# Four edits of order in a one-core decoder layer: first norm, last attention pair, loads of x, start of the down product

## The reference, cut to what matters

```python
q, k, v, hc, bc, cc = split(rms_norm(x, g_mix) @ w_in)      # 1024 columns each
q, k = rms_norm(q, q_norm), rms_norm(k, k_norm)             # per head of 64
attn = merged dilated attention of 16 heads, with a bias by distance
y = bc * short_conv(cc * hc)                                # three taps
h = x + concat(rms_norm(attn), rms_norm(y)) @ w_out
h = h + (silu(n @ w_gate) * (n @ w_up)) @ w_down            # n = rms_norm(h), width 5632
h = h + sigmoid(rms_norm(h) @ w_ple_gate) * (p @ w_ple_proj)
```

## Time and profile before

| what | value |
|---|---|
| median of 3 runs | 2536.05 us (2533.64 to 2537.11) |
| profiled execution | 2535.68 us, span 2534.1 us |
| TensorE busy | 2481.5 us, 98% of the span |
| DVE / ACT / POOL busy | 69% / 37% / 10% |
| mean granted TensorE clock | 0.992 of full speed |
| chain that ended last | PE 93%, DVE 3%, DMA 2%, issue 1%, ACT 1% |
| DMA | 324 MB, mean 128 GB/s |

### The profile page before, as it was taken

The page is one execution under the profiler, slowest core; times in us unless marked ns, Lnnn a source line. Parts: engine busy times, 40 slices in busy tenths (PEclk is TensorE's granted clock), DMA queues, the critical chain, the costliest instruction groups (busy, mean ns, idle before and its releaser), DMA issues.

```text
span 2534.1 us, 51880 instructions
## 1 busy us (share of the span) xinstructions
PE 2481.5 (98%) x20462; PEld 2467.8 (97%) x20462; DVE 1753.1 (69%) x2194; ACT 933.4 (37%) x1201; POOL 252.9 (10%) x281
## 2 busy tenths in 40 slices
PE   5999999999989999999999999999999999999998
PEld 5999999999989999999999999999999999999998
DVE  5576777777786899898888889888533322356433
ACT  4333333333432444444444444444322222233331
POOL 1111110111111000000000000000000000143000
PEclk8999999999999999999999999999999999999999
DMA  5343333333333423333433333343655443233331
GB/s 187 121 135 116 124 108 110 106 125 109 118 119 114 162 93 137 118 133 117 150 127 138 133 116 133 116 143 129 222 191 180 161 142 118 78 91 103 112 112 67
DMA packets 99741, 324.00 MB, mean 128 GB/s; under 512 B 18258, under 2 KB 18514, under 8 KB 99168
## 3 DMA queue, kind: packets, MB, share of 16 engines
q1 hardware_dynamic: 72144, 250.25, 30.2%
q0 software_dynamic: 26672, 70.69, 8.1%
q10 hardware_dynamic: 864, 2.24, 0.2%
HBM read 286.80 MB, written 40.65 MB: 129 GB/s over the span
## 4 chain that ended last, share of the span: by engine, by line
PE 93%; DVE 3%; DMA 2%; issue 1%; ACT 1%; POOL 0%; ACTq 0%; DVEq 0%; SPq 0%
PE acc L560 18%; PE acc L564 18%; PE acc L562 18%; PE acc L765 11%; PE acc L766 11%; PE acc L764 11%; DMA wraw<-in_w_down 1%; PE aux L571 1%; PE aux L609 1%; PE aux L653 1%; DVE wlo L1252 1%; PE aux L583 0%; PE aux L582 0%; PE aux L581 0%; PE aux L622 0%
## 5 line engine op out<-in xcount | busy, mean ns | idle before, releaser
L1252 DVE TENSOR_TENSOR wlo<-wraw,whi 128x1024 fp32r<-128x1024 f32 (+1 forms) x276 | 333.3, 1208 | 396.2 <-ACT whi L904 395.5
L904 ACT ACTIVATE whi<-wraw 128x1024 fp32r<-128x1024 f32 (+1 forms) x276 | 285.5, 1035 | 705.5 <-PE acc L564 651.7
L764 PE MATMUL acc<-xb_hi,whi 128*128 128x260 f32 x1228 | 347.7, 283 | 4.4 <-DVE xb_lo_t L1643 4.4
L765 PE MATMUL acc<-xa_lo,whi 128*128 128x260 f32 x1228 | 348.4, 284 | 0.0
L766 PE MATMUL acc<-xa_hi,wlo 128*128 128x260 f32 x1228 | 348.3, 284 | 0.0
L766 PE MATMUL acc<-xb_hi,wlo 128*128 128x260 f32 x1228 | 347.4, 283 | 0.0
L764 PE MATMUL acc<-xa_hi,whi 128*128 128x260 f32 x1228 | 346.8, 282 | 0.0
L560 PE MATMUL acc<-slots_a,whi 128*128 128x260 f32 x1536 | 313.3, 285 | 0.0
L564 PE MATMUL acc<-slots_a,wlo 128*128 128x260 f32 x1536 | 309.4, 283 | 0.0
L562 PE MATMUL acc<-slots_a,whi 128*128 128x260 f32 x1536 | 309.4, 283 | 0.0
L560 PE MATMUL acc<-slots_b,whi 128*128 128x260 f32 x1408 | 284.7, 284 | 4.8 <-ACT hid L1194 3.2
(11 more groups left out here) (290 smaller groups left out, 5087.0 us busy)
## 6 DMA issues: line engine op xcount, KB each, us to landing
wraw<-in_w_in SPq DMA_DIRECT2D x96, 512.0 KB, 3.6
blocks<-in_w_gate SPq DMA_DIRECT2D x88, 512.0 KB, 6.0
blocks<-in_w_up SPq DMA_DIRECT2D x88, 512.0 KB, 5.9
wraw<-in_w_down SPq DMA_DIRECT2D x48, 448.0 KB, 3.4
wraw<-in_w_out SPq DMA_DIRECT2D x32, 512.0 KB, 3.5
wraw<-in_w_ple_gate SPq DMA_DIRECT2D x32, 512.0 KB, 3.6
slots_b<-f_dram SPq DMA_DIRECT2D x28, 520.0 KB, 4.6
f_dram<-sig_t POOLq DMA_DIRECT2D x22, 520.0 KB, 3.2
```

The lines of the kernel that those rows point to most:

```text
L764: mm(to, w_h, hi, start=p == 0, stop=False)
L765: mm(to, w_h, lo, start=False, stop=False)
L904: on(whi[:, u % HILO, 0:width], wraw[:, u % RAW, 0:width], ACT.Copy).then_inc(s_whi, 1)
L1252: V.tensor_tensor(wlo[:, u % HILO, 0:width], wraw[:, u % RAW, 0:width], whi[:, u % HILO, 0:width].bitcast(F32), ALU.subtract).then_inc(s_w ...
```

## The change

- `X_SQUARES`: four groups of four tiles instead of five, five and six. The column sums move from behind unit 2 to behind unit 5, the transposes of the root from behind unit 4 to behind unit 6. q is copied like v and k, and k, q and v are scaled in place behind unit 6; `s_vk` becomes `s_vkq` (three steps).
- SP loads x0 ahead of the first weights and then the even pieces; ACT the odd ones. Before it was odd on SP and even on ACT.
- The attention of the last pair runs behind turns 3 to 14 instead of 2 to 13 on PE, ACT and DVE; what followed it in turns 12 and 14 is in 13 and 15. POOL's last squares move from turn 12 to 15. `load_values(KA - 1)` stays at POOL's turn 6.
- The first four units of the down product write the spare banks (T and O, S and D) and then the two accumulators. The tiles of chunk 1 are issued one behind each unit, from m = 5 on, the last three between the weights of the next chunk, which waits for its tiles in two parts.

```diff
-X_SQUARES = (range(0, 5), range(5, 10), range(10, KT))
+X_SQUARES = (range(0, 4), range(4, 8), range(8, 12), range(12, KT))
...
+    def first_down(m):
+        return (spare, spare_low, acc_of(0), acc_of(1))[m]
...
-                    load_x(1)
-                    load_x(3)
+                    load_x(2)
...
-                    load_x(5)
-                    load_x(7)
+                    load_x(4)
+                    load_x(6)
...
+        load_x(0)
         pair(FIRST, 0, first=True)
...
-            for n in {4: (0,), 5: (1,), 6: (2,), 7: (3, 4), 8: (5,), 9: (6,), 10: (7,), 11: (8, 9)}.get(
-                    m, (m - 2,) if m > 11 else ()):
-                if n == 7:
-                    sp.wait_ge(d_fhi, 16 * (PAIRS // 2))
-                load_hidden(1, n)
+            if m >= 5:
+                load_hidden(1, m - 5)
...
+                    if c == 1 and i == 0 and b > 0:
+                        load_hidden(1, 10 + b)
...
-                if a is None and g == 2:
+                if a is None and g == 5:
                     pe.wait_ge(s_bias, 1)
                     pe.wait_ge(s_xadd, KT - 1)
                     column_sums(x_sum).then_inc(s_nsum, 1)
-                if a is None and g == 4:
+                if a is None and g == 6:
                     pe.wait_ge(s_ninv, N_X)
...
-            if i == 3:
-                pe.wait_ge(s_read, T_CONV + 3)
-            if 2 <= i <= PAIR_UNITS + 1:
-                attention(KA - 1, i - 2, final=True)
-            if i == 14:
+            if 3 <= i <= PAIR_UNITS + 2:
+                attention(KA - 1, i - 3, final=True)
+            if i == KT - 1:
                 pe.wait_ge(s_sqs, SQ_ATTN)
...
+        pe.wait_ge(s_nroot, N_FFN)
         for b in range(4):
-            if b < 2:
-                pe.wait_ge(s_ev, 6 * PAIRS - 2 * (1 - b))
-            if b == 0:
+            if b >= 2:
                 pe.wait_ge(s_cp, 2 * PAIRS)
-            else:
-                pe.wait_ge(s_read, T_D + b - 1)
+                pe.wait_ge(s_ev, 6 * PAIRS)
...
-                scaled(q_t[:, :], 0, rstd).then_inc(s_read, 1)
-                if a is None:
-                    dve.wait_ge(s_read, 2)
-                    for tile in (v_t, k_t):
-                        V.tensor_tensor(tile[:, :], tile[:, :], rstd[:, :], ALU.mult).then_inc(s_vk, 1)
+                    scaled(q_t[:, :], 0, rstd).then_inc(s_read, 1)
+            if a is None and g == 6:
+                dve.wait_ge(s_xspread, 1)
+                V.tensor_copy(rstd[:, 0:SEQ], aux[:, BANK_S, :])
+                V.tensor_copy(rstd[:, SEQ:T], aux[:, BANK_D, 0:DEC]).then_inc(s_xwide, 1)
+                dve.wait_ge(s_xwide, 1)
+                dve.wait_ge(s_read, 3)
+                for tile in (k_t, q_t, v_t):
+                    V.tensor_tensor(tile[:, :], tile[:, :], rstd[:, :], ALU.mult).then_inc(s_vkq, 1)
...
             if i == 6:
                 load_values(KA - 1)
-            if i == 12:
+            if i == KT - 1:
                 pool.wait_ge(s_o, 2 * KA)
```

More of the change, by code:

```diff
@@ L337, in acc_of @@
         return acc[:, slot, :, 0:HALF]
-    spare = aux[:, BANK_T:BANK_O + 1, 0:HALF]
+    spare, spare_low = aux[:, BANK_T:BANK_O + 1, 0:HALF], aux[:, BANK_S:BANK_D + 1, 0:HALF]
     aux_sum = (aux.rearrange("p b f -> p (b f)")[:, 0:2 * (1024 - HALF)]
@@ L393, in build @@
     l_f0 = [sem(f"first_hidden_landed{n}") for n in range(DOWN[0][0])]
-    l_f = [sem(f"hidden_landed{c}") for c in range(CHUNKS)]
+    l_f = [[sem(f"hidden_landed{c}_{part}") for part in range(len(DOWN[c]))] for c in range(CHUNKS)]
     l_11, l_21, l_12 = sem("block11_landed"), sem("block21_landed"), sem("block12_landed")
@@ L672, in heads @@
                 else:
-                    pe.wait_ge(s_vk, 2)
+                    pe.wait_ge(s_vkq, 3)
                 pe.wait_ge(s_read, 6 * j + 3)
@@ L850, in _ @@
         for c in range(1, CHUNKS):
-            pe.wait_ge(l_f[c], 16 * sum(DOWN[c]))
             with pe.Fori(0, KT // 2) as i:
                 at = Span(U_CHUNK[c], 4, i)
+                pe.wait_ge(l_f[c][0], 16 * DOWN[c][0])
                 for b in range(2):
@@ L939, in heads @@
                 if a is None:
-                    act.wait_ge(s_vk, 2)
+                    act.wait_ge(s_vkq, 3)
                 on(sq[:, :], k_t[:, :], ACT.Square).then_inc(s_sq, 1)
@@ L974, in pair @@
                 split(at, g + HILO)
-                if a is None and g < 3:
+                if a is None and g < 4:
                     for t in X_SQUARES[g]:
                         square_x(t)
-                if a is None and g == 3:
+                if a is None and g == 5:
                     act.wait_ge(s_nsum, N_X)
@@ L1000, in _ @@
         act.dma_start(cols[:, :], gains).then_inc(l_gains, 16)
-        for g in range(0, PIECES, 2):
+        for g in range(1, PIECES, 2):
             act.dma_start(hid[:, g * XP:(g + 1) * XP, :], x_tiles[:, g * XP:(g + 1) * XP, :]).then_inc(l_x[g], 16)
@@ L1188, in _, with first_copy @@
         hidden_hi(PAIRS // 2 - 1, tmp[:, 2:4, :])
-        def first_copy(i, b):
+        def first_copy(i, b, source=None):
             m = i * 4 + b
             act.wait_ge(s_unit, m + (U_D + 1))
-            on(halves(hid[:, m, :]), acc_of(b % 2), ACT.Copy).then_inc(s_read, 1)
-        with act.Fori(0, KT // 4 - 1) as i:
+            on(halves(hid[:, m, :]), acc_of(b % 2) if source is None else source, ACT.Copy).then_inc(s_read, 1)
+        for b in range(4):
+            first_copy(0, b, first_down(b))
+            split(Span(U_D), HILO + b, DOWN[0][0] * P)
+        with act.Fori(1, KT // 4 - 1) as i:
             for b in range(4):
@@ L1384, in heads @@
                         V.tensor_tensor(x_sum, x_sum, tmp[:, t % 2, :], ALU.add).then_inc(s_xadd, 1)
-            if a is None and g == 3:
-                dve.wait_ge(s_nroot, N_X)
-                V.reciprocal(gsq[:, 0:QB], gsq[:, 0:QB])
-                V.reciprocal(gsq[0:DEC, QB:QB + 1], gsq[0:DEC, QB:QB + 1]).then_inc(s_ninv, 1)
-            if a is None and g == 4:
-                dve.wait_ge(s_xspread, 1)
-                V.tensor_copy(rstd[:, 0:SEQ], aux[:, BANK_S, :])
-                V.tensor_copy(rstd[:, SEQ:T], aux[:, BANK_D, 0:DEC]).then_inc(s_xwide, 1)
-                dve.wait_ge(s_xwide, 1)
             if a is None and g == 5:
@@ L1548, in _ @@
             dve.wait_ge(l_res[i % 2], 16 * (i // 2 + 1))
+            if i == KT - 1:
+                dve.wait_ge(s_sqs, SQ_CONV + 1)
             V.tensor_tensor(hid[:, m, :], act_t[:, :], res[:, i % 2, :], ALU.add).then_inc(s_h, 1)
@@ L1554, in _ @@
                 q_lo(KA - 1)
-            if 2 <= i <= PAIR_UNITS + 1:
-                attention(KA - 1, i - 2, final=True)
-            if i < KA - 1 or i == 12:
+            if 3 <= i <= PAIR_UNITS + 2:
+                attention(KA - 1, i - 3, final=True)
+            if i < KA - 1 or i == 13:
                 t = min(i, KA - 1)
@@ L1958, in _ @@
         pool.dma_start(old_passed, state_conv[0, :, 1, :]).then_inc(d_state, 16)
-        pool.wait_ge(s_vk, 2)
+        pool.wait_ge(s_vkq, 3)
         store_rows(0)
```

28 lines of the change are left out of this document (18 added, 10 removed).

## The result

The changed kernel takes **2522.8 us** (median of five runs, 2521.3 to 2524.8) against 2536.1 (five runs, 2533.6 to 2537.1): the ratio is 0.995, 95% interval 0.9939 to 0.9961. The forecast was 2522.9, the range 2514.5 to 2528.5. The profiled execution took 2521.28 us, with a span of 2519.7 us and a mean granted clock of 0.995 (0.992 before).

What follows compares the result with a forecast made beforehand. TensorE was taken as the bound (98% of the span), so only its standstills or lower clock could be won. 2535.7 - 13.7 + 5.0 - 4.1 = 2522.9 us, range 2514.5 to 2528.5.

Steps and rivals of the forecast that it cites:

- part 1: First norm: column sums no longer wait for squares and additions; the copy of `v_t` decides unit 4; gain 13.7 us.
- part 2: Last pair's attention one unit later: 2.3 us won, then a late residual tile 7 stalls step 5; loss 5.0 us.
- part 3: Down product: waits in the first units go, two of 1.3 and 1.2 us stay at units 6 and 7; gain 4.1 us.
- the start gains nothing by itself: First norm: TensorE's earlier start wins nothing, since the copy of `v_t` decides when unit 4 starts.
- at most 0.7: First norm: the new order of x moves everything behind tile 8, so also the copy of `v_t`, by at most 0.7 us.
- the tile: Last pair: residual tile 7, issued by POOL behind the cached values, lands at 765.7, 6.3 us after DVE wants it.
- (b): Last pair: the residual tile overtakes the values, landing after 3.0 us instead of 7.1; about 2518.9 us; chance 0.04.
- (a): Last pair: the residual tile is in time, part 2 keeps its 2.3 us; 2515.0 us; chance 0.11.
- (c): Slower than before: DVE doesn't catch up, TensorE waits in attention steps 5 to 9 at 1.2 GHz; 2551 us; chance 0.04.
- (d): First norm: wait behind the additions stays, squares interleaving with four splits; 13.7 shrinks to 4, 2532.6 us; chance 0.05.
- (e): First norm: no clock drop before unit 4; 2520.4 us; counted in the forecast's own spread, no separate chance.

Runs made afterwards that it cites:

- x_alone: Kernel before with only the new order and queues of the loads of x; 2535.26 us, ratio 0.9999.
- x_back: Changed kernel with the old order and queue of the tiles of x; 2524.38 us, ratio 0.9953.
- four_edits: Changed kernel with squares_ahead, values_turn8 and tiles_later edits, plus DVE reading unit 1 first in turn 1 of the output product; 2503.21 us.
- attn_alone: Kernel before with only the last pair's attention moved one unit later; 2540.44 us, ratio 1.0021.
- small_groups: Changed kernel with the first two groups of squares halved (groups of 2, 2, 4, 4, 4); 2526.42 us, ratio 0.9961.
- v_copy_first: Changed kernel with DVE's copy of v_t moved to the end of the start phase, once unit 1 is done; 2521.24 us, ratio 0.9939.
- squares_ahead: Changed kernel with v_copy_first's early copy, and six squares and their additions ahead of the split of unit 4; 2518.39 us, ratio 0.9928.
- tiles_later: Changed kernel with the hidden tiles of the second chunk started at turn 8 of the down product, not 5; 2520.85 us, ratio 0.9938.
- values_turn8: Changed kernel with the cached values' load at POOL's turn 8 instead of 6, behind residual tiles 7 and 8; 2515.54 us, ratio 0.9917.
- norm_alone: Kernel before with only the first-norm edit, loads of x in the old order; 2521.68 us, ratio 0.9948.

## Why the prediction was right, and where it was off

| term | forecast | in the two traces | part alone |
|---|---|---|---|
| part 1, first norm, with the order of x | -13.7 | -13.9 | -14.7 (norm), -1.1 (x) |
| part 2, last pair | +5.0 | +3.5 | +4.1 |
| part 3, down product | -4.1 | -3.5 | -3.2 |
| between | 0 | -0.6 | |
| sum | -12.8 | -14.4 | |

The forecast stood on the profiled execution before (2535.7); the difference of the two profiled executions is 14.4 us and that of the medians 13.3, so 1.1 of the 1.6 us by which the sum was short is spread of single executions. That the median met the forecast within 0.1 us is luck: the terms are off by up to 1.5 us, and the runs lie 3.5 us apart. The row "between" is clock as well: behind the `xb_lo_t` wait TensorE worked 4.3 us at 1.2 GHz in the trace before and 2.9 us in the one after, which is 0.7 us by the pair times of the earlier trace rows.

**Part 1 held, link by link.** The copy was to end at 41.2 and ended at 41.3. Unit 5 was to end at 55.2, and the sums start at 54.98. The additions, forecast at 51, end at 50.84. The wait before unit 4 is 4.4 us, not 3.2, and this is no contradiction: unit 3 ended 1 us before the 38.0 of the working, because the first unit's clock was back at 2.4 GHz by 15.2, and since the copy decides, the earlier end went into the wait. The sentence "the start gains nothing by itself" is true of TensorE's start (x_alone: the sums at 49.23 against 49.39) but would mislead alone: x_back suggests that the order of x moves the weights of unit 4, some 0.8 us, which the working had as "at most 0.7" in the place of the copy.

**Part 2 has the right mechanism, and a clock term that varies from one execution to the next.** The wait before unit 3 was forecast at 4.3 us and is 4.34. The profile doesn't put it down to DVE, as I had said it would, but to "issue". The DVE row that ends it is the read of unit 1:

```profile
704.03 0.69 DVE L1262 TENSOR_TENSOR tmp<-acc,rstd 128x520 f32<-128x520 f32 x1
```

It ends at 704.72 and unit 3 starts at 704.82; four_edits moves this row, and the wait follows it. In the changed kernel's trace the clock is the term that was off. I had taken it as low already at 716.6, as in the earlier trace rows, and as low for most of unit 3; it fell only 4.2 us after the stop and was back after 3.3 us of work. Unit 3 and attention step 0 were done 3.4 us earlier than in the kernel before (13.9 us of part 1 taken off), not 2.3. The rest of the chain moved with it: the key reductions end at 741.2 (forecast 756.8, which is 742.9 when the 13.9 us of part 1 are taken off), the tile lands at 749.7 (751.8), DVE waits 5.8 us (6.3), TensorE 5.4 (6.2). In the other direction, the stretch at 1.2 GHz behind that wait was 4.8 us long: 2.1 us lost by the pair times of the earlier trace rows, where I had put 1.2. In all 3.5 us, not 5.0; the lower end of the spread of that part, 3, had been given for an earlier tile.

But one trace can't correct this term. Seven traces have the moved attention with the values' load still at turn 6 (the changed kernel, attn_alone, x_back, small_groups, v_copy_first, squares_ahead, tiles_later). From the sums of the output product to the end of the `xb_lo_t` wait they take 217.9 to 220.1 us, where the kernel before takes 214.65 (213.9 to 214.7 in the four traces without the edit): a loss of 3.3 to 5.4 us, 4.5 on average. In the changed kernel and tiles_later the stretch at 1.2 GHz around unit 3 is 3.4 us long; in the other five it is 6.8 us, and in attn_alone TensorE worked 4.5 us in it, for most of unit 3, as forecast. So the forecast of 5.0 lies inside what the same edit costs from one execution to the next.

**The rule on completion order.** The page "DMA: Bandwidth & Descriptors" of the Trainium skill, section "Queues, rings and completion order", says that completion isn't first in, first out for one issuing engine; it says so of the queues of SP and ACT. The tile here went through POOL's. It was issued 1.2 us behind 1 MB of values and took 6.7 us, the same as the values, and 3.3 us without them. By the rule, as rival (b) had it, the kernel would have taken 2518.9 us. Overtaking could have saved 3.4 of DVE's 5.83 us; the 7.2 us of values_turn8 are the price of the place in POOL's list and not of the order of completion alone. These rows don't show that a transfer never overtakes another, only that this one didn't.

**Part 3.** Waits of 1.3 and 1.2 us at units 6 and 7 were forecast, 1.33 and 1.61 measured, with no drop. The second is 0.4 us too small. I had taken one hidden tile less ahead of the weights of unit 8 as 2.6 us; its split starts at 1814.38 and still waits for weights, 1.9 us earlier than before when the 11.0 us by which the stage starts earlier are taken off, and tiles_later, with none ahead, ends most of this wait. The waits in units 0 to 3 are gone, as forecast.

**The rivals.** (a), the tile in time, and (b) are excluded by the DVE wait of 5.83 us. (c), a backlog that isn't caught up, didn't come: TensorE's list has no other wait in the steps behind it. (d), a wait at the sums as long as before, is excluded by the row at 54.98; but small_groups shows that its mechanism, squares behind splits that wait for weights, is real: with five groups in place of four it cost 3.6 us. (e), no drop before unit 4, didn't come.

## What to carry to other kernels

When a step is moved in a software pipeline, list what its results release on the issuing queues, and read in the trace what stands behind that instruction there: here a move that took 2.3 us off a wait cost 4.1 us, because a load that waits for the moved step stood ahead of an unrelated tile in POOL's list, and changing their places gave 7.2 us. A small operation that frees a buffer belongs where its input is ready, but look at the next waiter first: pieces that hang on other transfers don't move with it. And a gain early in the kernel can be given back in part where work meets transfers at another time; subtract the times of the same events to find the place. Before a term is corrected by one trace, read it in the others that have the same code: here the loss of one and the same edit differed by 2 us from one execution to the next, and most of that was clock.

## What the runs showed of the hardware

- The fall to 1.2 GHz can come after TensorE has started again. In v_copy_first it stood from 48.6 to 51.35, and the clock fell at about 53.1; in squares_ahead it stood from 1809.8 to 1812.14, and the clock fell at about 1813.3. The windows of squares_ahead:

```profile
1812.00:1813.00 1.00, 0.86 (x7) 0.87 (x8) 0.24 (x1) 0.31 (x2) 0.00 (x0) 1.00 0.31 123
1813.00:1814.00 1.00, 1.00 (x8) 1.00 (x8) 0.63 (x1) 0.82 (x2) 0.00 (x0) 0.67 0.49 117
1816.00:1817.00 1.00, 1.00 (x7) 1.00 (x7) 0.33 (x1) 0.12 (x1) 0.00 (x0) 0.63 0.94 357
```

- The time from a stop to the fall isn't constant: 2.1, 3.3 and 4.2 us in the changed kernel, 2.3 us in four_edits. The best comparison is the `xb_lo_t` wait, which is 4.2 us long in all fourteen traces: the clock fell from 1.5 us (norm_alone, stopped at 902.9, first window) to 4.5 us (four_edits, stopped at 891.2, second window) after the stop.

```profile
904.00:905.00 1.00, 0.00 (x0) 0.00 (x0) 1.00 (x2) 0.73 (x1) 0.00 (x0) 0.72 0.00 0
895.00:896.00 1.00, 0.58 (x3) 0.58 (x4) 1.00 (x2) 0.00 (x0) 0.00 (x0) 0.84 0.77 201
```

- The length of a stop doesn't decide alone whether the clock falls. The down product of squares_ahead had a fall behind a stop of 2.36 us, that of small_groups none behind a stop of 2.36 us (restart at 1816.43, window below); x_back had none behind 2.03 us. The kernel before had one behind a stop of 1.74 us that ended at 1828.54 and followed others, and the changed kernel none behind 1.61.

```profile
1816.00:1817.00 1.00, 0.57 (x4) 0.58 (x5) 0.53 (x1) 0.30 (x1) 0.00 (x0) 1.00 1.01 403
```

- The work done at 1.2 GHz before the clock was back varied as well: 3.0 us before it was back in x_back's first pair, 4.5 in the changed kernel's, and 5.7 us behind the wait of the earlier trace rows in the kernel before (721.1 to 726.8).
- The first unit's slow phase also varies from one execution to the next, by the times between its matmuls (a pair every 0.43 us, then every 0.24): up to 15.2 us in the changed kernel, 15.5 in v_copy_first, 17.9 in squares_ahead. That moves the end of unit 3 by 1 us.
